# Expert inputs of a one-core decoder step: rows moved by DMA instead of turned on TensorE, norm factor put into the gate function

## What is computed

```
def rmsnorm(x, g):
    y = xf * lax.rsqrt(jnp.mean(xf * xf, axis=-1, keepdims=True) + EPS)
    return (y * g.astype(jnp.float32)).astype(x.dtype)

def hier_moe(h, wg, bg, we, be, w_gate, w_up, w_down):     # h = rmsnorm(x, norm_moe)
    ...        # top-1 group of 4, then top-2 experts of 4 inside it: gate (288 x 16)
    a = jnp.einsum('nd,edf->nef', t, w_gate)
    u = jnp.einsum('nd,edf->nef', t, w_up)
    act = jax.nn.silu(a) * u * gate[..., None].astype(h.dtype)
    out = jnp.einsum('nef,efd->nd', act, w_down)
```

## Time and profile before

| what | value |
|---|---|
| median of the runs | 1483.19 us |
| profiled execution | 1484.51 us, its span 1482.8 us |
| TensorE busy | 1427.7 us, 96% |
| VectorE, ScalarE, GpSimd busy | 555.9, 190.1, 796.8 us |
| mean DMA rate over the span | 254 GB/s |
| DMA in the last 12 of 40 slices | 99% busy or more, 421 to 423 GB/s |
| one round of two experts on TensorE while it leads (down starts 1034.55, 1090.30) | 55.7 us |
| same where the weights lead (waits at 1211.34, 1270.99) | 59.7 us |
| a copy of the gather, 128 x 16 | 213 ns on GpSimd |

### The profile page before, as it was taken

One profiled execution on the slowest core, in us unless ns is written; L12 is line 12 of the kernel. 1 busy time (PEld: TensorE's weight loads), 2 busy tenths in 40 slices (PEclk: granted clock), 3 DMA queues, 4 the chain that ended last, 5 costly groups with the idle time before them and its releaser, 6 DMA issues.

```text
span 1482.8 us, 25563 instructions
## 1 busy us (share of the span) xinstructions
PE 1427.7 (96%) x9308; PEld 1089.8 (73%) x9308; DVE 555.9 (37%) x1067; ACT 190.1 (13%) x392; POOL 796.8 (54%) x1453
## 2 busy tenths in 40 slices
PE   6999999999999999999999999979999999999997
PEld 6999999998889999998777799963334334344344
DVE  3546578829575342222111342151112122122123
ACT  5100321000000010003222200051000000000003
POOL 3777587979987757763444467512451440522500
PEclk8999999999999999999999999989999999999999
DMA  8344344445654444464788744747999999999993
GB/s 256 124 161 142 107 150 129 155 145 176 208 167 162 142 166 143 146 236 191 299 318 310 248 152 154 293 189 323 421 421 422 422 422 422 422 422 422 422 422 140
DMA packets 106120, 377.07 MB, mean 254 GB/s; under 512 B 12421, under 2 KB 12421, under 8 KB 76290
## 3 DMA queue, kind: packets, MB, share of 16 engines
q1 hardware_dynamic: 103778, 371.68, 65.8%
q10 hardware_dynamic: 2272, 4.42, 0.9%
HBM read 369.30 MB, written 6.77 MB: 254 GB/s over the span
## 4 chain that ended last, share of the span: by engine, by line
PE 83%; DMA 10%; DVE 3%; ACT 2%; issue 1%; SPq 1%; POOL 0%; POOLq 0%; ACTq 0%; DVEq 0%
PE ps L840 40%; PE ps L897 13%; PE ps L1184 11%; DMA tiles<-in_expert_w_up 8%; PE ps L1250 4%; PE ps L1214 3%; PE ps L966 2%; DMA tiles<-in_expert_w_down 2%; PE ps L790 1%; PE ps L1201 1%; PE ps L984 1%; PE ps L974 1%; PE ps L1005 1%; DMA A<-in_norm_final 1%; PE ps L1032 0%
## 5 line engine op out<-in xcount | busy, mean ns | idle before, releaser
L749 POOL COPY A<-A 128x16 f32 x952 | 146.1, 213 | 289.4 <-issue 289.3
L840 PE MATMUL ps<-hT,tiles 128*128 128x144 f32 x1792 | 295.3, 288 | 3.4 <-ACT A L1406 1.5
L840 PE MATMUL ps<-A,tiles 128*128 128x144 f32 x1792 | 262.0, 286 | 0.8 <-DVE A L2003 0.7
L840 PEld LDWEIGHTS ps<-hT,tiles 128*128 128x128 f32 x1792 | 251.6, 191 | 5.0 <-issue 2.6
L840 PEld LDWEIGHTS ps<-A,tiles 128*128 128x128 f32 x1792 | 237.0, 190 | 1.9 <-DVE A L2003 0.9
L702 POOL TENSOR_TENSOR tiles<-tiles 128x512 f32<-128x512 f32 x88 | 117.3, 1333 | 173.4 <-DMA tiles<-in_w_in 70.4
L840 PE MATMUL ps<-tiles 128*128 128x144 f32 x960 | 171.1, 287 | 0.0
L1184 PE MATMUL ps<-tiles,A 128*64 128x512 f32 x512 | 147.0, 601 | 13.2 <-DMA A<-in_expert_w_up 6.4
L840 PEld LDWEIGHTS ps<-tiles 128*128 128x128 f32 x960 | 140.4, 191 | 0.0
L897 PE MATMUL ps<-tiles,mT 128*128 128x256 f32 x512 | 132.9, 382 | 1.0 <-ACT kv_stage L1440 1.0
L1709 DVE COPY pair_sums<-ps 128x144 f32<-128x144 f32 x44 | 13.5, 308 | 300.4 <-PE ps L840 300.4
(11 more groups left out here) (350 smaller groups left out, 1698.6 us busy)
## 6 DMA issues: line engine op xcount, KB each, us to landing
tiles<-in_expert_w_down SPq DMA_DIRECT2D x56, 1024.0 KB, 22.4
tiles<-in_w_in SPq DMA_DIRECT2D x40, 1024.0 KB, 5.1
tiles<-in_expert_w_gate SPq DMA_DIRECT2D x32, 1024.0 KB, 22.1
tiles<-in_expert_w_up SPq DMA_DIRECT2D x32, 1024.0 KB, 22.5
A<-in_expert_w_up SPq DMA_DIRECT2D x24, 1024.0 KB, 25.2
tiles<-in_xa_w_k SPq DMA_DIRECT2D x16, 1024.0 KB, 5.1
tiles<-in_w_out SPq DMA_DIRECT2D x16, 1024.0 KB, 5.1
tiles<-in_xa_w_q SPq DMA_DIRECT2D x16, 1024.0 KB, 5.1
```

Of the source, the lines that this page charges most:

```text
L749: m = nc.gpsimd.tensor_copy(xe[:, :, at + n:at + n + 1], h_moe_or_zero[:, :, bass.ds(token, 1)])
L840: return mm(one(u + mp, x, TH), w[:, kp, mp, :], rhs, start=(first and g == 0 and kp == 0), stop=(g == 3 and kp == 1), skip_group_check=True)
```

## The change

- The gate and up tiles are read in another row order: partition p of tile g holds features 512 g + 4 p + k. So a feature keeps its group g of four blocks and only changes partition and block within it.
- All token turns go. Instead SyncE issues 32 transfers (`move_rows`) from `hT` to `h_rows`, 16 for three quarters of the features and 16 for the last. They stand after tiles 8 and 9; tiles 10 and 11 come behind them, tiles 12 and 13 (in hT's place) also wait until they have landed.
- The gathers read `h_rows`. Empty slots now name token 0 instead of a zero column. The slots of the first expert are shared 20 (GpSimd), 24 (ScalarE), 20 (VectorE).
- The norm factor is no longer in the tokens. `take_roots` (6 matmuls) brings it per slot, ScalarE copies it to `slot_root` and the silu uses it as its scale; the up side takes it through the gates, one more product on VectorE.
- The logits have a unit of their own. The places unit, whose bank 4 now holds the first roots, is read out by VectorE (one count) and ScalarE (one count).
- VectorE gathers before it makes the gates instead of after.
- `keep_running` is called with `WARM` = 0, so it issues nothing.

```diff
-POOL_SLOTS, ACT_SLOTS = 24, 48
+POOL_SLOTS, ACT_SLOTS = 20, 44
+WARM = 0
...
-        h_moe_or_zero, at = cut(0, DB, 1 + T)
...
+        h_rows, at = cut(0, DB, T)
...
+        first_slot_roots = bank(UNIT["places"], 0)[0:C, 0:2]
+        slot_roots = ps[0:C, 6, T + 4:T + 6]
...
-        e_gate = a["expert_w_gate"][0].rearrange("e (p g k) f -> e g p k f", k=KT, p=P)
+        e_gate = a["expert_w_gate"][0].rearrange("e (g p k) f -> e g p k f", k=KT, p=P)
...
                 elif m >= 12:
-                    after_event(sp, EVENT["h_tok_rest"] + 1)
+                    after_event(sp, EVENT["router"])
+                    sp.wait_ge(rows_moved, 16 * 2 * KT * KT)
...
+            def move_rows(first, n):
+
+                sp.wait_ge(h_ready, 4 * HREADY["moe"] + first + n)
+                for old in range(KT):
+                    for new in range(KT):
+                        src = hT[new:P:KT, :, :].rearrange("p (g b) t -> p g b t", b=KT)[:, first:first + n, old, :]
+                        dst = h_rows[P // KT * old:P // KT * (old + 1), :, :].rearrange("p (g b) t -> p g b t", b=KT)[:, first:first + n, new, :]
+                        sp.dma_start(dst, src).then_inc(rows_moved, 16)
+
             branch_tiles(0, 0, range(8))
-            branch_tiles(1, 8, range(MOE_SLOTS - 8))
+            branch_tiles(1, 8, range(2))
+            sp.wait_ge(tile_used, TILE["moe"])
+            move_rows(0, 3)
+            move_rows(3, 1)
+            branch_tiles(1, 8, range(2, MOE_SLOTS - 8))
...
-                        m = nc.gpsimd.tensor_copy(xe[:, :, at + n:at + n + 1], h_moe_or_zero[:, :, bass.ds(token, 1)])
+                        m = nc.gpsimd.tensor_copy(xe[:, :, at + n:at + n + 1], h_rows[:, :, bass.ds(token, 1)])
...
+            def take_roots(out):
+
+                for s in range(2):
+                    for c in range(3):
+                        n = own_rows[c]
+                        m = mm(out[:, s:s + 1], pick[0:n, c, C * s:C * s + C], h_rstd[0:n, c:c + 1], start=(c == 0), stop=(c == 2))
+                return m
+
+            pe.wait_ge(tokens_numbered, 1)
+            pe.wait_ge(pick_ready, 1)
+            number_slots(first_slot_sums)
+            take_roots(first_slot_roots).then_inc(unit_done, 1)
...
                 pe.wait_ge(pick_ready, plus(n // 2 + 1, i, 1))
+                take_roots(slot_roots)
                 number_slots(slot_sums)
...
-            turn_back_chunk(1, UNIT["h_moe_rest"])
...
-            read_out(pe, UNIT["h_moe_rest"])
+            keep_running(BRANCH_BANK + 1, WARM)
             read_out(pe, UNIT["places"])
-            pe.wait_ge(h_moe_out, 3)
             pe.wait_ge(xe_ready, 1)
...
-            def gate_branch(t, s, i):
-
+            def gate_branch(t, s, n, i):
+
+                act.wait_ge(slot_root_out, plus(n, i, 1))
                 after_tile(act, TILE["moe"] + t + 7, i, 24)
-                fn(silu[0:C, :], ps[0:C, 4 + s, :], ACT.Silu).then_inc(silu_ready, 1)
+                fn(silu[0:C, :], ps[0:C, 4 + s, :], ACT.Silu, scale=slot_root[0:C, s:s + 1]).then_inc(silu_ready, 1)
...
-            gate_branch(0, 0, None)
-            gate_branch(8, 1, None)
+            after_event(act, EVENT["root_0"])
+            roots_out(first_slot_roots)
+            u = UNIT["places"]
+            act.wait_ge(slot_root_out, 1)
+            act.sem_inc(half_free[u % 2], 1)
+            gate_branch(0, 0, 1, None)
+            gate_branch(8, 1, 1, None)
             slots_numbered(slot_sums, EVENT["moe_0"] + 1, None, 1)
+            act.wait_ge(silu_ready, 2)
+            roots_out(slot_roots)
...
+            dve.wait_ge(slots_out, 1)
+            dve.wait_ge(rows_moved, 16 * 2 * KT * KT)
+            for first in range(ACT_SLOTS, C, 16):
+                for n, token in enumerate(tokens_of_slots(mybir.EngineType.DVE, 0, first, min(16, C - first))):
+                    at = first + n
+                    m = v.tensor_copy(xe[:, :, at:at + 1], h_rows[:, :, bass.ds(token, 1)])
+            m.then_inc(xe_third_part, 1)
             after_event(dve, EVENT["counts"])
-            v.tensor_copy(tab[:, 0, :], bank(u, 3)[:, 0:NE]).then_inc(half_free[u % 2], 2)
+            v.tensor_copy(tab[:, 0, :], bank(u, 3)[:, 0:NE]).then_inc(half_free[u % 2], 1)
...
+            then(tt(G(11), G(11), h_rstd[:, 0:3].unsqueeze(2).broadcast_to([P, 3, 4]), ALU.mult))
```

More of the change, by code:

```diff
@@ L472, in tokens_of_slots @@
             _, tokens = nc.values_load_multi_w_load_instructions(
-                slot_row(p, first, n), engines=[engine], min_val=0, max_val=T,
-                skip_runtime_bounds_check_because="a slot's sum over the tokens holds at most one token's number, 1 to T")
+                slot_row(p, first, n), engines=[engine], min_val=0, max_val=T - 1,
+                skip_runtime_bounds_check_because="a slot's sum over the tokens holds at most one token's number, 0 to T - 1")
             return tokens
@@ L1110, in _, with keep_running @@
             own_rows = (P, P, NB * ST)
[L1112 to L1124, removed]
-                    m = nc.tensor.transpose(out(b), (h_tok[:, c, :] if c < 2 else h_sam[0:rows, :])[:, b * P:(b + 1) * P],
-                                            ident[0:rows, 0:rows])
-                m.then_inc(unit_done, 1)
-            start_unit(pe, u)
-            for g in range(3):
-                route(g)
-            start_unit(pe, UNIT["h_tok"])
-            turn_tokens(0, range(12))
-            route(3).then_inc(unit_done, 1)
-            turn_tokens(0, range(12, 16)).then_inc(unit_done, 1)
+            start_unit(pe, u)
+            for g in range(4):
+                m = route(g)
+            m.then_inc(unit_done, 1)
+            def keep_running(b, times):
+                for n in range(times):
+                    wait_moe_tile(pe, n // KT)
+                    mm(ps[:, b, :], ident[:, :], moe_tile(n // KT)[:, n % KT * TW:(n % KT + 1) * TW], start=True, stop=True)
+            u = UNIT["logits"]
+            start_unit(pe, u)
             pe.wait_ge(logits_in, 1)
@@ L1142, in _ @@
             m.then_inc(unit_done, 1)
-            for c in range(1, 3):
-                start_unit(pe, UNIT["h_tok"] + c)
-                turn_tokens(c, range(DB)).then_inc(unit_done, 1)
-            def turn_back_chunk(c, unit):
-                start_unit(pe, unit)
-                turn_back(c, lambda b: bank(unit, b // 4)[:, b % 4 * P:(b % 4 + 1) * P])
-            turn_back_chunk(0, UNIT["h_moe"])
+            keep_running(4 * (UNIT["logits"] % 2), WARM and WARM + 2)
             u = UNIT["places"]
@@ L1545, in slots_numbered, with roots_out @@
                 copy(slot_row(p, 0, 2 * C), sums).then_inc(slots_out, 1)
-            act.wait_ge(token_rstd_ready, 1)
-            for c in range(3):
-                tokens_out(c)
-            after_event(act, EVENT["h_moe"])
-            turned_back(0, UNIT["h_moe"])
+            def roots_out(roots):
+                copy(slot_root[0:C, :], roots).then_inc(slot_root_out, 1)
             act.wait_ge(gate_in, 2)
@@ L2064, in _ @@
             v.tensor_copy(rstd[:, 0, :], bank(u, 0)[:, 0:T]).then_inc(logits_in, 1)
+            dve.wait_ge(logits_in, 1)
+            dve.wait_ge(stat_out, 1)
+            dve.sem_inc(half_free[u % 2], 2)
+            u = UNIT["logits"]
             dve.wait_ge(token_root, 1)
```

69 lines of the change are left out of this document (17 added, 52 removed).

## The result

The kernel after the change takes **1506.45 us** (median of 4 runs, 1504.28 to 1507.85), the one before 1483.62 (4 runs, 1482.83 to 1484.46). The ratio is 1.0152, with a 95% interval of 1.0135 to 1.0170: slower by 1.5%. The prediction was 1483.4 with a range of 1481.4 to 1486, so it was wrong; its rival of 1489.4 was also far too low.

The account below looks back on a forecast made before the run. The unbroken weight stream was taken to bound the kernel, so only its start counts: slot numbers 4.8 us before the old release, +5.26 for ScalarE's other copies, net +0.2 at the branch, giving 1483.4 us, range 1481.4 to 1486.

Parts of the forecast that it names:

- rival of 1489.4: Row moves into 32 partitions: at 160 ns per piece everything behind is 6.0 us later, 1489.4 us; chance 0.08.
- The stream never stops, so only its start can move the end: Expert weight stream: 178 tiles take 442 us unbroken from 1008.03, so a shift of the first load shifts the end.
- the rate behind it is 422 GB/s: Sign of being right: after the first load behind the gap, at about 1008.2, weights still stream at 422 GB/s.
- The term for the loop body: Expert loop: six more root matmuls per expert pair, 1.8 us on TensorE; 57.5 still fits the stream's 59.7, so no cost.
- TensorE keeps waiting 24 us: End of the expert stage: from 1330.69 on TensorE was read as waiting 24 us for each tile of weights.
- 32 take 11 to 15 us: SyncE's issue of the row moves from 968.7, at 0.33 to 0.48 us each, ending at 980 to 984.
- gathers that begin after 991: Sign of being wrong: token gathers that start after 991 and wait for the moves, instead of near 990.7.
- The fit of 2.0 us a transfer: Trainium skill's DMA cost, 2.0 us plus bytes at 436 GB/s; in series the 32 moves would take 69 us.
- the moves are late: Rival: row moves take turns in their 32 partitions; at 160 ns per piece 6.0 us later, 1489.4 us; chance 0.08.
- The wait that takes its place: First expert branch: TensorE waits for ScalarE's root copy behind all 56 gather copies, starting at 999.4 against 999.24 before.
- Clock at the branch … I take the same as before: Start of first branch: lower TensorE clock lasts 3.1 us as before; up to 1.6 us more was possible but not added.
- the last rival: Longer stretch at the lower clock: 3.1 us more at half speed, +1.6, 1485.0 us; counted within no change.

Follow-up runs that it names:

- e1: Kernel after the change, GpSimd's zeroing of wr cut into 18 memsets instead of 1 (17 more instructions ahead of its expert loop): 1486.92 us, ratio to before 1.0016.
- e2: Kernel before the change, GpSimd gathering 20 of its first slots instead of 24 (8 instructions fewer ahead of its loop): 1506.19 us, ratio 1.0157.
- f1: e1's kernel, with ScalarE copying the first two experts' roots out behind its first 24 gather copies instead of all 56: 1480.93 us, ratio to before 0.9981.
- e3: Kernel before the change with only the new row order of gate and up tiles, tokens left in the old order: 1484.37 us, ratio 1.0000.
- g1: e1's kernel with the edits of f1 and f2, plus 4 idle TensorE matmuls before the places and 3 before the first branch: 1476.93 us, ratio to before 0.9953.
- e1b: Kernel after the change with 6 zeroing memsets on GpSimd instead of 1, so 5 more instructions: 1503.94 us, one run.
- g2: Kernel before the change with the zeroing done by 113 memsets instead of 1 (112 more GpSimd instructions): 1505.69 us, ratio 1.0145.
- f2: e1's kernel, with the 32 row moves issued as 16 of 128 pieces each: 1483.58 us, ratio to before 0.9997.

## Why the prediction was wrong

- **The failed step: "The stream never stops, so only its start can move the end", with "the rate behind it is 422 GB/s".** I took the rate of the stream as given for any program, and asked only what the change does to its start. I never counted how the engines' programs grow or shrink, nor read the rows of the instruction queues. The stream never stopped for fifteen parts of each tile, but the sixteenth came up to 17 us later, and the round went from 59.7 to 62.9 us. The two profiles put 19.6 of 23.3 us there, and e1 and e2 show GpSimd's refetched loop as the cause. No rival named it. The term for the loop body (roots, +1.8 us on TensorE) was rightly given no cost: e1's rounds are 59.64.
- **A reading of the earlier trace rows**: "TensorE keeps waiting 24 us" is wrong. The 24 us run from a load's issue to its landing. TensorE stood still for 13.9 of the 276.9 us in that stretch. No number of the forecast used it.
- **"32 take 11 to 15 us"**: failed, 21.3. I priced a move's issue by that of a tile load, 0.33 to 0.48; it was 0.66. Moves landed at 991.4 instead of 983 to 986.5, and held the gathers by 2.1, which is the prediction's own sign of being wrong ("gathers that begin after 991"). The 2.3 us for a landing stands in no row; from issue to landing the moves took 1.8 to 3.7 us, median 2.6. The fit of 2.0 us a transfer that the prediction quotes from the Trainium skill is given there for transfers that GpSimd issues; these were SyncE's, and 32 of them in 22.5 us did overlap. Pieces took 65 ns where I had 63; their number was right and not the limit. The rival "the moves are late" came true, not by its mechanism (pieces taking turns) and at a third of its price.
- **"The wait that takes its place"**: right. The branch waited for ScalarE's root copy at the end of 56 gather copies; 999.4 became 1001.5 through the moves alone. (The 0.1 for two semaphore hops has no row of its own; the copy ended at 1001.4 and the branch began at 1001.50.) f1 shows it by taking the wait away.
- **"Clock at the branch … I take the same as before"**: mis-sized in the profiled execution. The lower level lasted until about 1007.5, 6 us instead of 3.1, and from the branch's start to the load it took 10.25 us instead of 8.79: +1.5, the 1.6 of the last rival. That the longer rest is the cause is not shown. The profile of e1, with the same rest, has 3.9 us at the lower level and 9.18 to the load; that of e3, with the TensorE program of before, has 4.9 and 9.79. So the length of this stretch varies by about 2 us between executions that share TensorE's program, with either program. g1 shows the price.
- The job table came before the slot, as predicted (SyncE waited another 2.5 us for TensorE behind it); places, picks and slot numbers were within 0.3 us; contiguous tiles gave nothing (e3); the roots in the loop were hidden (e1).
- Sum for the profiled executions: 0.2 predicted + 2.1 (moves) + 1.5 (clock) = 3.8, against 3.7 measured, + 19.6 in the stream.

## What to carry to other kernels

When a stream of DMA sets the time, read the instruction queues of the page before and after: a loop that is fetched again in each pass shows there as packets that were not there. Count the instructions of a loop body and of what stands in front of it, and when a harmless edit costs a per cent or two, shift the loop by a few instructions before believing any other cause. A mean share and a mean rate over 16 DMA engines can read full while one of them is late; the step of the chain from round to round cannot. And before crediting a clock effect to an edit, look at how much the same stretch varies between executions of kernels that share its program.

## What the runs showed of the hardware

- A GpSimd loop of 277 instructions was not fetched again when it started 0 to 3 (before) or 8 to 11 (e1) instructions behind the inferred boundary, but by five 8 KB packets a pass wherever it reached into a fourth block: 4 to 9 instructions earlier (after, e1b, e2) and 112 later (g2). In after, GpSimd stood still for 5.6 us at the branch back, against 0.27 before. How many blocks the engine holds is not shown.
- Each such packet of about 0.31 us put one DMA engine 0.62 us behind. Why twice its own time is open. So is what decides which engine that is.
- Issuing an SBUF to SBUF move from SyncE took a median of 0.60 us, one every 0.64 to 0.65 us, whether it carried 32 or 96 pieces (36 or 108 KB, after) or 128 (144 KB, f2). A few took over 1 us, which makes the means 0.66 and 0.71.
- Pieces of 1,152 bytes took 65 ns on average in after, and 116 ns in f2, where the DMA share was 1.09.
- The lower TensorE clock (0.50) lasted 3.1 to 6.0 us from the branch's start in before, e1, e3 and after, and not in the order of TensorE's idle time just before: 3.1 after 6.1 us, 3.9 after 11.2, 4.9 after 6.3, 6.0 after 11.0.
